# Latent attention computed on tokens, and two smaller rearrangements, in a transformer kernel on one Trainium2 core

## What is computed

```python
q = (rms_norm(c_q, q_lora_g) @ w_uq).reshape(B, S, 8, 96)
kv = (rms_norm(c_kv, kv_lora_g) @ w_ukv).reshape(B, S, 8, 128)
k_nope, v = kv[..., :64], kv[..., 64:]
k = concatenate([k_nope, broadcast(k_r)], -1)
q, k = rms_norm(q, q_g), rms_norm(k, k_g)
q = concatenate([q[..., :64], rotary(q[..., 64:], pos)], -1)
k = concatenate([k[..., :64], rotary(k[..., 64:], pos)], -1)
o = softmax(q k^T * 96 ** -0.5) v
x = x + concatenate([pool_mixer(u), o], -1) @ w_out_e
```

## Time and profile before

| | |
|---|---|
| runs | 1937.0, 1933.84, 1936.37 us; median 1936.37 |
| profiled execution | 1935.33 us, of which the trace spans 1933.5 |
| mean granted TensorE clock | 0.984 |
| busy share of the span: PE, DVE, ACT, POOL | 96%, 66%, 60%, 22% |
| instructions | 33004 |
| moved by DMA | 312 MB, mean 161 GB/s |

### The profile page before, as it was taken

The page is one execution under the profiler, slowest core; times in us unless marked ns, Lnnn a source line. Parts: engine busy times, 40 slices in busy tenths (PEclk is TensorE's granted clock), DMA queues, the critical chain, the costliest instruction groups (busy, mean ns, idle before and its releaser), DMA issues.

```text
span 1933.5 us, 33004 instructions
## 1 busy us (share of the span) xinstructions
PE 1858.0 (96%) x11332; PEld 1620.2 (84%) x11332; DVE 1281.3 (66%) x1922; ACT 1166.7 (60%) x1913; POOL 421.9 (22%) x447
## 2 busy tenths in 40 slices
PE   7888999999979999999999989999999999889998
PEld 6765988889759888888888988888988888678887
DVE  6756777676577676666666866666566566666665
ACT  4435656554366565568746859854588545659853
POOL 1120342122023320101213141212021120441212
PEclk9988999999989999999999999999999999999999
DMA  6411436557435365555644546563655646125562
GB/s 236 147 44 45 163 121 206 186 185 203 153 83 175 109 198 186 187 186 183 206 174 139 166 141 189 184 219 125 191 183 189 211 140 197 67 77 185 185 215 79
DMA packets 86765, 312.11 MB, mean 161 GB/s; under 512 B 10369, under 2 KB 15617, under 8 KB 86401
## 3 DMA queue, kind: packets, MB, share of 16 engines
q1 hardware_dynamic: 86368, 309.01, 48.3%
q10 hardware_dynamic: 288, 1.64, 0.2%
HBM read 309.56 MB, written 1.05 MB: 161 GB/s over the span
## 4 chain that ended last, share of the span: by engine, by line
PE 88%; DVE 6%; ACT 2%; issue 2%; POOL 1%; DMA 0%; POOLq 0%; SPq 0%; DVEq 0%; ACTq 0%
PE pt L469 41%; PE pt L470 21%; PE pt L463 5%; PE pt L465 5%; PE pt L464 5%; PE pt L583 1%; PE pt L587 1%; PE pt L585 1%; DVE w_lo L1687 1%; PE pt L1051 1%; PE pt L834 1%; PE pt L625 1%; ACT w_hi L1153 1%; PE pt L653 1%; PE pt L697 1%
## 5 line engine op out<-in xcount | busy, mean ns | idle before, releaser
L1687 DVE TENSOR_TENSOR w_lo<-raw,w_hi 128x1024 fp32r<-128x1024 f32 (+2 forms) x548 | 706.5, 1290 | 294.9 <-ACT w_hi L1153 286.9
L1153 ACT ACTIVATE w_hi<-raw 128x1024 fp32r<-128x1024 f32 (+2 forms) x548 | 598.5, 1094 | 407.4 <-PE pt L470 229.9
L469 PE MATMUL pt<-in_both,w_hi 128*128 128x512 f32 x2103 | 744.1, 399 | 0.8 <-DVE in_both L2167 0.8
L470 PE MATMUL pt<-in_both,w_lo 128*128 128x256 f32 x2103 | 590.2, 281 | 0.0
L469 PEld LDWEIGHTS pt<-in_both,w_hi 128*128 128x128 f32 x2103 | 395.1, 188 | 100.1 <-DVE in_both L2167 1.4
L469 PE MATMUL pt<-act_both,w_hi 128*128 128x512 f32 x1309 | 463.4, 399 | 0.0
L470 PEld LDWEIGHTS pt<-in_both,w_lo 128*128 128x128 f32 x2103 | 397.1, 189 | 0.1
L470 PE MATMUL pt<-act_both,w_lo 128*128 128x256 f32 x1309 | 366.6, 280 | 0.0
L469 PEld LDWEIGHTS pt<-act_both,w_hi 128*128 128x128 f32 x1309 | 245.8, 188 | 60.8 <-issue 0.9
L470 PEld LDWEIGHTS pt<-act_both,w_lo 128*128 128x128 f32 x1309 | 247.0, 189 | 0.2
L2346 POOL TENSOR_TENSOR act_both<-scr,act_both 128x256 f32 x88 | 100.2, 1138 | 498.2 <-ACT act_both L1576 498.2
(11 more groups left out here) (271 smaller groups left out, 2330.3 us busy)
## 6 DMA issues: line engine op xcount, KB each, us to landing
raw<-in_fi SPq DMA_DIRECT2D x176, 512.0 KB, 3.6
raw<-in_ff SPq DMA_DIRECT2D x128, 512.0 KB, 3.6
raw<-in_fo SPq DMA_DIRECT2D x64, 704.0 KB, 4.0
raw<-in_dq SPq DMA_DIRECT2D x24, 512.0 KB, 4.3
raw<-in_mq SPq DMA_DIRECT2D x16, 512.0 KB, 3.4
raw<-in_mo SPq DMA_DIRECT2D x16, 512.0 KB, 3.7
raw<-in_rg_u SPq DMA_DIRECT2D x10, 512.0 KB, 3.3
raw<-in_rg_y SPq DMA_DIRECT2D x10, 512.0 KB, 3.7
```

The costliest lines, as they stand in the source:

```text
L469: nc.tensor.matmul(pt[:, b, :], lhs_hi, both.rearrange("p t s -> p (t s)"), start=start, stop=False)
L470: return nc.tensor.matmul(pt[:, b, 0:S], lhs_lo, both[:, 0, :], start=False, stop=stop)
L1153: nc.scalar.activation(w_hi[:, u.slot(), w], raw[:, u.slot(), w], ACT.Copy).then_inc(hi_split, 1)
L1687: v.tensor_tensor(w_lo[:, u.slot(), w], raw[:, u.slot(), w], w_hi[:, u.slot(), w].bitcast(F32), ALU.subtract).then_inc(lo_split, 1)
```

## The change

Latent attention: q and the keys are made on tokens (128 tokens on the partitions, all heads along them), two token halves one after the other, `ukv` between them. ACT squares straight from the banks, DVE sums along the partitions (`q_rstd`), the rotation is a few wide instructions on DVE with tables brought to tokens by PE (`kr_turn`, inside `in_pool`). PE then transposes q and k of all heads to features ahead of the loop. The gains and the scale of the scores are folded into ACT's copy of q. In the loop two heads form a pair: scores of a pair ahead, four buffers of probabilities, two banks of transposes, two output banks, products with the values for a pair at a time, and `out_e` in three units abreast, seven of its eight steps (`out_e_abreast`) between the loop's last ones. The pool branch moves: its first product behind the latent projections, its second behind the scores of pair 1, its copies to ACT, its low halves into DVE's step 1. One split of `in_pool` is held back on DVE. POOL has no part in the latent attention any more.

Recurrence: `lru_lo` moves from POOL to DVE. Dilated attention: 38 products whose result nobody reads (`keep_busy`, 256 columns, into bank 7) at the first groups.

The core of the diff; left out are semaphores, views of buffers, functions whose names say what they do, and the removed code, which is described above:

```diff
...
-          ("uq", 2, 768, 8), ("ukv", 1, 1024, 6), ("out_e", 8, 1024, 8)]
+          ("uq", 2, 768, 4), ("ukv", 1, 1024, 4), ("out_e", 8, 1024, 8)]
...
+            def kr_turn():
+                pe.wait_ge(acc_free, ACC0["in_t"] + 4)
+                for t in range(2):
+                    nc.tensor.matmul(pt[:, 7, MLA_ROPE * t:MLA_ROPE * t + MLA_ROPE], big[rot_rows, 20, t * P:t * P + P],
+                                     ident[rot_rows, rot_rows], start=True, stop=True)
+                pe.wait_ge(rotary_tables, 1)
+                for side in range(2):
+                    for n, (angle, table) in enumerate(((cos, ident_g), (sin, rot_g))):
+                        for t in range(2):
+                            at = 64 + 128 * side + 64 * n + MLA_ROPE * t
+                            mm = nc.tensor.matmul(pt[:, 7, at:at + MLA_ROPE], angle[:, t * P:t * P + P], table[side],
+                                                  start=True, stop=True)
+                mm.then_inc(kr_on_tokens, 1)
+            project_tokens("in_pool", within=lambda i: latent_sums() if i == 0 else kr_turn() if i == 1 else None)
...
+            pe.wait_ge(act_ready, ACT0["pool"])
+            queries(1)
+            u = UNIT0["ukv"]
+            pe.wait_ge(lo_split, u + 1)
+            for part in range(2):
+                if part:
+                    pe.wait_ge(kr_copied, 1)
+                w = slice(part * 512, part * 512 + 512)
+                for t in range(2):
+                    o, ts = pt[:, 4 + 2 * part + t, :], slice(t * P, t * P + P)
...
+                    nc.tensor.matmul(o, act_hi[:, 10, ts], w_lo[:, u % RING, w], start=False, stop=True
+                                     ).then_inc(ukv_done, 1)
             pe.wait_ge(acc_free, ACC0["in_pool"] + 2)
+            queries(0)
+            pe.wait_ge(v_copied, 2)
...
+            def mla_scores(p):
+                if p < 2:
+                    pe.wait_ge(query_dims, 2 * p + 2)
+                    pe.wait_ge(key_dims_dve, p + 1)
+                else:
+                    pe.wait_ge(key_dims_act, p - 1)
+                    pe.wait_ge(exp_ready, h_mla + 2 * p - 2)
+                for h in (2 * p, 2 * p + 1):
+                    for t in range(2):
+                        mm = nc.tensor.matmul(pt[:, h % 4, t * S:t * S + S], big[0:MLA_QK, 4 + h, t * P:t * P + P],
+                                              big[0:MLA_QK, 12 + h, :], start=True, stop=True)
+                    mm.then_inc(scores_ready, 1)
...
+            def mla_value(p):
+                v = chunks(big, 20, 4)
+                pe.wait_ge(turned_copied, h_mla + 2 * p + 2)
+                pe.wait_ge(act_ready, ACT0["mla"] + max(p - 1, 0))
...
+            pe.wait_ge(q_roped, 1)
+            for p in range(4):
+                mla_query_turn(p)
+            pe.wait_ge(k_made, 1)
+            mla_key_turn(0)
+            mla_key_turn(1)
+            mla_scores(0)
+            mla_key_turn(2)
+            mla_key_turn(3)
+            mla_scores(1)
             pe.wait_ge(pool_read, 1)
             for g in range(4):
                 mm = nc.tensor.matmul(pt[:, 6 + g // 2, (g % 2) * S:(g % 2) * S + S],
                                       gain("poolw", g * P, P), pooled[:, g * S:g * S + S], start=True, stop=True)
             mm.then_inc(mixed, 1)
...
+            mla_scores(2)
+            mla_turn(0)
+            mla_turn(1)
+            mla_scores(3)
+            mla_value(0)
+            mla_turn(2)
+            mla_turn(3)
+            mla_value(1)
+            mla_turn(4)
+            mla_turn(5)
+            pe.wait_ge(exp_ready, h_mla + 7)
+            out_e_abreast(0)
+            mla_value(2)
+            mla_turn(6)
+            out_e_abreast(1)
+            mla_turn(7)
+            out_e_abreast(2)
+            out_e_abreast(3)
+            out_e_abreast(4)
+            mla_value(3)
+            out_e_abreast(5)
+            out_e_abreast(6)
+            project("out_e", 8, acts, from_act("pool"), wide=3, begun=7)
...
+            for _ in range(6):
+                nc.tensor.matmul(pt[:, 7, 0:S], in_hi[:, 0, 0:P], in_hi[:, 1, :], start=True, stop=True)
...
+            def keep_busy(n):
+                for _ in range(n):
+                    nc.tensor.matmul(pt[:, 7, 0:S], in_hi[:, 0, 0:P], in_hi[:, 1, :], start=True, stop=True)
             h0 = HEAD0["dil"]
             for s in range(PAIRS):
                 dil_lead(s)
+                if s in (1, 2):
+                    keep_busy(5)
                 if s >= 3:
                     dil_turn(2 * s - 5)
                 dil_scores(s)
+                if s < 2:
+                    keep_busy(11)
...
@@ scalar engine @@
+            queries(1)
             for t in range(2):
...
+                act.wait_ge(ukv_done, t + 1)
+                nc.scalar.activation(k_square[t], pt[:, 4 + t, :], ACT.Square).then_inc(k_squared, 1)
+            act.wait_ge(acc_free, ACC0["in_pool"] + 2)
+            queries(0)
             for u in range(3):
                 act.sem_inc(unit_used, 1)
...
+            act.wait_ge(q_squared, 4)
+            act.wait_ge(q_copied, 4)
+            act.wait_ge(v_copied, 2)
+            for n in range(6):
+                act.sem_inc(acc_free, 1)
+            act.wait_ge(qk_summed, 1)
+            nc.scalar.activation(q_rstd, q_rstd, ACT.Sqrt, bias=eps_qk).then_inc(qk_root, 1)
+            nc.scalar.activation(warm, eps_qk, ACT.Exp)
+            act.wait_ge(mixed, 1)
...
+            for p in range(4):
+                mla_query_dims(p)
+            mla_exps(0)
+            mla_key_dims(2)
+            mla_exps(1)
+            mla_key_dims(3)
+            mla_exps(2)
+            mla_copy(0)
+            mla_exps(3)
+            mla_copy(1)
+            act.wait_ge(mixed, 2)
+            for g in range(4):
+                nc.scalar.activation(act_hi[:, g, :], pt[:, 6 + g // 2, (g % 2) * S:(g % 2) * S + S],
+                                     ACT.Copy, scale=gain("ps", g)).then_inc(act_hi_ready, 1)
+            split(Pos(UNIT0["uq"] + RING))
+            for s in (2, 3):
+                mla_exps(2 * s)
+                mla_copy(2 * s - 2)
+                mla_exps(2 * s + 1)
+                mla_copy(2 * s - 1)
+                mla_high(s - 2)
+                split(Pos(UNIT0["uq"] + RING + s - 1))
+            mla_copy(6)
+            mla_copy(7)
+            mla_high(2)
+            mla_high(3)
+            units("out_e", after=next_input("xa0"))
...
@@ vector engine @@
+                if q == 2:
+                    dve.wait_ge(kr_on_tokens, 1)
+                    v.tensor_copy(kr_tok, pt[:, 7, 0:2 * MLA_ROPE].rearrange("p (t d) -> p t d", t=2))
+                    v.tensor_copy(rope[:, 0:256], pt[:, 7, 64:320]).then_inc(kr_copied, 1)
+                    dve.wait_ge(kr_copied, 1)
...
+            tokens("in_pool", chunks(big, 0, 4), 512, after_split=latents, hold=True)
...
+            dve.wait_ge(q_squared, 2)
+            summed(1, 0, q_square[1], MLA_QK)
+            for t in range(2):
+                dve.wait_ge(k_squared, t + 1)
+                summed(t, 1, k_square[t], MLA_NOPE)
+            for t in range(2):
+                dve.wait_ge(ukv_done, t + 3)
+                v.tensor_copy(chunks(big, 20, 4)[:, t * 512:t * 512 + 512], pt[:, 6 + t, :]).then_inc(v_copied, 1)
+            split(Pos(UNIT0["in_pool"] + 3 + RING))
+            dve.wait_ge(q_squared, 4)
+            summed(0, 0, q_square[0], MLA_QK)
+            link(v.memset(warm, 1.0))
+            k_sums = q_rstd[:, :, 8:16]
+            v.tensor_tensor(k_sums, k_sums, kr_sum.unsqueeze(2).broadcast_to([P, 2, MLA_HEADS]), ALU.add
+                            ).then_inc(qk_summed, 1)
+            dve.wait_ge(q_copied, 4)
...
+            mla_key_dims(0)
+            mla_key_dims(1)
+            mla_maxes(0)
+            mla_maxes(1)
+            for s in (1, 2, 3):
+                mla_maxes(2 * s)
+                mla_norms(2 * s - 2)
+                mla_maxes(2 * s + 1)
+                mla_norms(2 * s - 1)
+                if s == 1:
+                    dve.wait_ge(act_hi_ready, ACT0["pool"] + 4)
+                    for g in range(4):
+                        v.scalar_tensor_tensor(out=act_lo[:, g, :], in0=pt[:, 6 + g // 2, (g % 2) * S:(g % 2) * S + S],
+                                               scalar=gain("ps", g), in1=act_hi[:, g, :].bitcast(F32),
+                                               op0=ALU.mult, op1=ALU.subtract).then_inc(act_ready, 1)
+                if s == 3:
+                    mla_low(0)
+                split(Pos(UNIT0["uq"] + RING + s - 1))
+            mla_norms(6)
+            mla_norms(7)
+            mla_low(1)
+            mla_low(2)
+            mla_low(3)
+            units("out_e", before=add_to_x(), after=input_low("xa0", x))
...
+                if kind == "y" and 5 <= i <= 8:
+                    lru_lo(i - 5)
...
+            lru_lo(RC // 2 - 1)
...
@@ gpsimd @@
```

(36 more changed lines are left out.)

382 lines of the change are left out of this document (194 added, 188 removed).

## The result

The changed kernel takes **1905.9 us** (median of 4 runs, 1903.4 to 1908.7) against 1936.2 (4 runs, 1933.8 to 1937.0): ratio 0.984, 95% interval 0.9819 to 0.9861, 30.3 us less. Forecast were 1911.5 and a range of 1904 to 1919. Direction and range held; the gain was 5.4 larger than the forecast 24.9.

A forecast was written before the change was run, and what follows sets the result against it. TensorE, 88% of the chain, was taken as the bound, so only its waits and half-clock stretches could shrink, worst in latent attention; 21.5 + 2.3 + 1.1 = 24.9 us off 1936.4 gave 1911.5, range 1904 to 1919.

The forecast's parts named there:

- part 1: Latent attention in its new instruction order: gain 26.5 us at full clock, 21.5 after charges, range 14 to 28.
- Until k is made: Latent attention ahead of the scores: narrow products add 2.4 us, pool mixing ends at 116.1, k is made by 118.9.
- Scores: Latent attention: scores of pair 0 by 122.1, pair 1 by 124.95, pair 2 by 128.45, turn 0 by 129.05.
- The added wait: Latent loop: DVE idles 5.3 us before the pool's low halves until ACT has made the high ones, at 132.85.
- Tail: End of latent attention: last `out_e` steps and value 3 end at 160.7; additions start there instead of at 187.28.
- The clock: Latent loop: TensorE's clock falls near 143, recovers some 8 us later, charged 3 us; narrow products in `in_pool` charged 1.
- Part 2: Recurrence: low halves on DVE instead of POOL gain 2.3 us, bounds 0 and 3.
- Part 3: Dilated attention: 38 filler products gain 1.1 us if they hold the clock, bounds +1.5 and -1.
- A: Rival: the clock holds in the latent loop or hops are shorter; gain 30 us, 1906.5; chance 0.22.
- B: Rival: clock oscillates, or is half from the first scores, in the latent loop; gain 19 us, 1917; chance 0.16.
- C: Rival: narrow products drop the clock, which stays down until `out_e`; 8.5 us slower, 1945; chance 0.03.
- D: Rival: the latent attention's gain is eaten downstream or not there; about 1926 us; chance 0.05.

The follow-up runs named there:

- experiment 4: Changed kernel with DVE's low halves of the pool and the split behind them one loop step later: 1904.0 us; 1.93 less to `out_e`'s first addition.
- experiment 5: Changed kernel with 44 filler products in TensorE's gaps of the latent loop: 1902.1 us; 0.9 less to `out_e`'s first addition.
- experiment 2: Changed kernel without the 38 filler products of the dilated attention: 1905.0 us.
- experiment 1: Changed kernel run again without any edit: 1902.7 us, with the kernel before at 1938.9 beside it.
- experiment 6: Changed kernel with the value products of a pair of heads made one head after the other instead of in turns: 1901.8 us.

## Why the prediction was right, and where its size was off

The direction rested on part 1 and on its account of the order on each engine. Its waits came where it put them; parts 1 and 2 gained more than forecast, part 3 less. Point by point:

- *Until k is made.* The narrow products cost 2.3 (97.75 to 100.09; forecast 2.4), the queries began at 105.67 (105.8), the pool mixing ended at 116.2 (116.1), the first score came at 120.35, exactly as forecast.
- *Scores.* Pair 1 was done at 124.76 (124.95), pair 2 began at 126.48. Turn 0 began at 128.21 behind it; the account had it end at 129.05.
- *The added wait.* 5.29 (5.3), up to 132.52 (132.85). Its price, which the account took in only through its order, is 1.0 to 1.9 (experiment 4).
- *Tail.* Forecast end at full clock 160.7, measured first addition 159.86 with 13.6 us of half clock in it, which cost 0.9, so at full clock 159.0. Of the 1.7 us between, value 3 explains 0.7 (4 products at 0.43 were priced, which is right for one head alone; two heads run side by side, and the row shows 1.08 for all), and another 0.7 that the first unit's addition does not wait for the other two units' last step.
- **The step that failed is "The clock".** That it would fall was right; it fell 6 us earlier and stayed longer (forecast near 143 for 8 us, measured 137.0 for 13.6). Its charge was not: 3 were charged, 0.9 were paid (experiment 5). The same paragraph had TensorE at work for only 40% of this stretch, but put half of the 6 us of doubled work on the path all the same, without asking which products stand there; the chain above has only the short turns. For the narrow products 1 was charged, 3 at 30%. A fall behind them came in 4 of the 12 traces of the changed kernel and its variants (in experiment 2's from 101.2 to 104.6) and cost 1.6, so the chance was right, the price about twice too high and the average 0.5; the profiled execution had none. The 1 us for missed hops was not needed. Clock 2.1, narrow products 1, hops 1 and the 1.7 of the tail make 5.8 of the 5.7 by which the measured 27.2 exceed the forecast 21.5.
- *Part 2.* 2.6 measured (2.06 behind split 312 and 0.5 before), 2.3 forecast. The 0.5 is what the upper bound of 3 allowed for, that the splits are quicker with POOL silent.
- *Part 3.* 0.3 on average, 1.1 forecast. The step that failed is "if they hold the clock": in 4 of 9 traces, the profiled execution's among them, they moved the fall one pair on. So the sign "no clock below 1 in the dilated attention" did not come either.

By sum: 27.2 + 0.5 + 2.6 + 0.3 = 30.6, where the medians differ by 30.3 and in experiment 1's set by 36.2; what makes the 0.5 (`out_e`'s end) is open. Forecast were 21.5 + 2.3 + 1.1.

The rivals: A gave nearly the right number, 1906.5, by luck, since the clock did fall; nor were the hops shorter, what stood in for them is the cheap half clock and the 1.7 of the tail. B fell twice: there was one fall and not an oscillation from the first pair on, and half clock was cheap. So the rule of the Trainium skill, TensorE: Matmul & The Clock Gate, section "A second HAM failure mode: psum-queue depth-cycling", was not borne out in the size that I gave it: the pairs up to 129 stayed at 1.00 and the loop fell once for 13.6 us. Of C the start came, a fall behind the narrow products in 4 of 12 traces, but the clock was back after 3.4 us and did not stay down. Of D nothing came: at split 300 the changed kernel is still 27.0 us ahead.

## What to carry to other kernels

Where engines pass small pieces to and fro, write the order of each engine out with the trace's durations before pricing the clock: half clock costs only what lies on the chain, here 0.9 us of 13.6. Look in the same account for an engine that stands in its program order while its next inputs lie ready; here the order alone was worth 10.6 us of the stretch, another third of what the change had given, and kept the clock without fillers. A filler that only shortens one gap can pass the fall on to the next; judge it over several executions, and judge any step of a few us by its own stretch of the trace.

## What the runs showed of the hardware

- Instructions of an f32 product that move 256 columns start every 0.22 us with 128 loaded columns and 96 or 128 partitions, one at a time; with 64 loaded columns and one head alone it is 0.22 as well (kernel before, four in 1.08). With the products of two heads that write different halves of the partitions they start in twos every 0.22 (eight in 1.08), whether the heads alternate or follow one another (experiment 6).
- The same uninterrupted products run at one of two rates, 66.6 or 67.8 us for splits 339 to 363, at the same granted clock; which one belongs to the execution.
- The 20 instructions of the narrow products, which load 128 columns on 32 partitions and move 32, cost 0.12 us apiece (2.3 in all). That is as much as a transpose's instruction, which loads 128 and moves 128 (eight take 1.04 in the changed kernel, 0.11 between starts).
